# GpSimd's quarter sums in the input projection of a hybrid encoder layer, done in two runs per token block

## What is computed

```python
h = rmsnorm(x, norm1_w)
proj = h @ w_in                        # q, k, v, z, xBC, dt_f, dt_b
q = rmsnorm(q per head, q_norm_w) * 64 ** -0.5
k = rmsnorm(k per head, k_norm_w)
att = neighbourhood_attention(q, k, v, rpb)
xBC = silu(depthwise_conv(xBC, conv_w, conv_b))      # five taps
ssm = two-way chunked scan over xBC, gated by silu(z)
x = x + concatenate([att, ssm]) @ w_out
h2 = rmsnorm(x, norm2_w)
y = x + (silu(h2 @ w_gate) * (h2 @ w_up)) @ w_down
```

## Time and profile before

| | |
|---|---|
| median of 3 executions | 3426.62 us (3421.67 to 3434.69) |
| the profiled execution | 3428.72 us, of which its span is 3426.6 us |
| TensorE busy | 3205.6 us, 94% |
| VectorE, ScalarE, GpSimd busy | 2031.9 us (59%), 1390.9 us (41%), 720.0 us (21%) |
| granted TensorE clock, mean over the span | 0.972 |
| input projection | from the start to about 790 us |

### The profile page before, as it was taken

One profiled execution on the slowest core, in us unless ns is written; L12 is line 12 of the kernel. 1 busy time (PEld: TensorE's weight loads), 2 busy tenths in 40 slices (PEclk: granted clock), 3 DMA queues, 4 the chain that ended last, 5 costly groups with the idle time before them and its releaser, 6 DMA issues. The chain is left out here.

```text
span 3426.6 us, 48500 instructions
## 1 busy us (share of the span) xinstructions
PE 3205.6 (94%) x16456; PEld 2762.9 (81%) x16456; DVE 2031.9 (59%) x3070; ACT 1390.9 (41%) x2610; POOL 720.0 (21%) x683
## 2 busy tenths in 40 slices
PE   7999999996999779979979999999999998999999
PEld 6877777774777558968858999999999997887887
DVE  3446556473666578974447555755576665555655
ACT  3333434354667535542214333433343333434443
POOL 5453534412333236742220000000000000000000
PEclk9999999998999989989989999999999999999999
DMA  8686858567433032236656454745475555666776
GB/s 267 232 292 219 327 179 330 201 232 132 87 83 75 29 86 68 66 128 197 204 183 229 148 162 150 235 151 159 150 227 175 174 174 201 215 220 236 272 248 214
DMA packets 458415, 630.02 MB, mean 184 GB/s; under 512 B 133120, under 2 KB 271920, under 8 KB 453856
## 3 DMA queue, kind: packets, MB, share of 16 engines
q1 hardware_dynamic: 431808, 522.36, 48.0%
q0 software_dynamic: 23600, 100.80, 8.4%
q10 hardware_dynamic: 2880, 5.24, 0.4%
HBM read 451.25 MB, written 177.75 MB: 184 GB/s over the span
## 5 line engine op out<-in xcount | busy, mean ns | idle before, releaser
L65 PE MATMUL u_acc<-u_h_hi,u_w_hi 128*128 128x448 f32 (+1 forms) x1848 | 657.5, 356 | 23.9 <-DVE u_h_lo L2333 21.4
L66 PE MATMUL u_acc<-u_h_lo,u_w_hi 128*128 128x448 f32 (+1 forms) x1848 | 656.9, 355 | 0.0
L67 PE MATMUL u_acc<-u_h_hi,u_w_lo 128*128 128x448 f32 (+1 forms) x1848 | 656.8, 355 | 0.0
L65 PEld LDWEIGHTS u_acc<-u_h_hi,u_w_hi 128*128 128x128 f32 x1848 | 348.0, 188 | 44.3 <-issue 22.9
L67 PEld LDWEIGHTS u_acc<-u_h_hi,u_w_lo 128*128 128x128 f32 x1848 | 347.9, 188 | 18.5
L66 PEld LDWEIGHTS u_acc<-u_h_lo,u_w_hi 128*128 128x128 f32 x1848 | 348.0, 188 | 18.3
L2577 ACT CAST d_hi<-d_raw 128x896 fp32r<-128x896 f32 (+1 forms) x231 | 225.0, 983 | 279.4 <-PE d_acc L67 140.9
L460 DVE TENSOR_TENSOR i_w_lo<-i_raw,i_w_hi 128x2048 fp32r<-128x2048 f32 x60 | 158.0, 2633 | 295.7 <-ACT i_w_hi L332 295.7
L65 PE MATMUL d_acc<-d_hi 128*128 128x512 f32 x770 | 302.0, 392 | 17.2 <-DVE d_lo L2598 13.0
L2598 DVE TENSOR_TENSOR d_lo<-d_raw,d_hi 128x896 fp32r<-128x896 f32 (+1 forms) x231 | 252.0, 1132 | 111.1 <-ACT d_hi L2577 105.7
L66 PE MATMUL d_acc<-d_lo,d_hi 128*128 128x512 f32 x770 | 301.4, 391 | 0.0
(11 more groups left out here) (256 smaller groups left out, 6411.4 us busy)
## 6 DMA issues: line engine op xcount, KB each, us to landing
u_w_lo<-w_ops SPq DMA_DIRECT2D x264, 256.0 KB, 2.9
i_raw<-w_in_dram SPq DMA_DIRECT2D x60, 1024.0 KB, 6.8
u_w_raw<-w_ffn_dram SPq DMA_DIRECT2D x198, 256.0 KB, 3.1
d_raw<-wd_ops SPq DMA_DIRECT2D x132, 256.0 KB, 5.7
d_raw<-hid_ops SPq DMA_DIRECT2D x154, 192.0 KB, 6.1
d_raw<-w_down_dram SPq DMA_DIRECT2D x99, 256.0 KB, 5.7
i_ops<-w_ffn_dram POOLq DMA_DIRECT2D x44, 512.0 KB, 6.3
w_ops<-i_ops POOLq DMA_DIRECT2D x22, 1024.0 KB, 6.9
```

The costliest lines, as they stand in the source:

```text
L65: pe.matmul(out, w_hi, x_hi, start=first, stop=False, skip_group_check=resumed)
L66: pe.matmul(out, w_hi, x_lo, start=False, stop=False, skip_group_check=resumed)
L67: return pe.matmul(out, w_lo, x_hi, start=False, stop=last, skip_group_check=resumed)
```

## The change

GpSimd's pieces of a block stand in two runs. `OPS_AT` gives begin, middle and end for each block. The pieces from `begin` to `middle` stand where the seven stood; then GpSimd waits until bank 3 holds v, that is until slot 7's matmuls are done, and only then makes those from `middle` to `end`. The gains of q still follow behind all of them. The runs are 4 + 4, 4 + 3, 4 + 3, 4 + 3 and 4 + 0 pieces instead of 7, 7, 7, 7 and 5. Nothing is computed otherwise.

```diff
-    OPS = 7
+    OPS_AT = ((0, 4, 8), (8, 12, 15), (15, 19, 22), (22, 26, 29), (29, 33, 33))
...
             def token_block(tb, more, conv):
-                for n in range(OPS * tb, min(OPS * (tb + 1), 3 * FP)):
+                begin, middle, end = OPS_AT[tb]
+                for n in range(begin, end):
+                    if n == middle:
+                        pool.wait_ge(acc_ready[3], tb * USES + USE[6] + 1)
                     if n + 1 < 3 * FP:
                         load_ops(n + 1)
                     make_ops(n)
```

## The result

| | before | after |
|---|---|---|
| median | 3430.7 us (4 runs) | 3483.0 us (4 runs, 3470.3 to 3489.9) |
| ratio | | 1.0157, 95% interval 1.013 to 1.0184 |
| profiled execution, its span | 3428.7, 3426.6 us | 3487.1, 3485.0 us |
| granted TensorE clock | 0.972 | 0.965 |

A forecast was written before the change was run, and what follows sets the result against it. TensorE, busy 94% of the span, bounds the kernel. Stalls 61.5 plus restarts 8.8 minus saving 19.2 give +51.1 us on 3428.7, that is 3479.8; less 2.1 to the median, 3477.7 us, 8 times in 10 within 3453 to 3505.

The forecast's parts named there:

- The saving: Blocks 1 to 3, slot 7 to slot 10: no piece beside the taps, waits for v and clock loss gone, 19.2 us.
- The stalls: TensorE waits at slot 10 for q's first gain: 12.6 us in blocks 1 to 3, 23.7 in block 0, together 61.5.
- Landings: GpSimd waits between pieces behind the wait for stores to land: 6.5, 4.5 and, in block 0 alone, 4.0 us.
- meetings with `w_lo`: Slots 8 to 10: VectorE's `w_lo` lengthens GpSimd's sums, charged 3.0 us, one full meeting and half of another.
- The port rule: VectorE instructions with two SBUF inputs and GpSimd instructions reading SBUF exclude each other; slots 8 to 10, 5.8 us of meetings.
- my third rival: Every `w_lo` meets a sum in full, 2.8 us more in each of four blocks: 3488.9 us, chance 0.15.
- The clock: TensorE's restarts at the low clock level after the waits at slot 10: four at 2.2 us, 8.8 us.
- In block 4 the wait for v: TensorE's wait for v in block 4, 2.6 us, stays after the change.
- The first: The gains don't gate slot 10, or are in time: -19.2 us, 3407.4 us, chance 0.03.
- The second: Short stalls, +24 us, partly paid back by four later waits for `h_lo` vanishing: 3439 us, chance 0.06.
- The fourth: Landings stay as long as in the busy slots or longer, the high end: 3533 us, chance 0.06.

The follow-up runs named there:

- Run 1: The changed order, but GpSimd's multiplication of q by its gains left out and VectorE counting up `ev_ready`; 3416.0 us, ratio 0.9956 against the kernel before.
- run 4: The changed kernel with one piece behind the wait in blocks 1 to 3 and block 0 left whole; 3412.5 us, ratio 0.9952 against the kernel before.
- run 5: The changed kernel with two pieces behind the wait in blocks 1 to 3 and block 0 left whole; 3413.8 us, ratio 0.9958 against the kernel before.
- run 10: The changed kernel with four pieces put beside the taps in blocks 1 to 3 and every piece's sums left out; 3405.5 us, ratio 0.9924 against the kernel before.
- run 8: The changed kernel again, unchanged, for a second profile; 3477.7 us in 6 runs, ratio 1.0141 against the kernel before.
- run 3: The changed kernel's numbers of pieces with the new wait taken out; 3431.1 us, ratio 0.9994 against the kernel before.
- run 7: The kernel before again, unchanged, for a second profile; 3417.9 us in one execution.

## Why the prediction was right

**The saving.** It was put at 19.2 us, all of it in blocks 1 to 3. Run 1 gave -0.44%, that is -15 us, after some 5 us given back at the start of block 1; run 4 gave -0.48%, -16 us. The first matmul of the attention came at 776.0 and 774.9 us in runs 4 and 5, against 799.7 and 789.3 before. The mechanism is shown by runs 4 and 10: freeing slot 7's taps takes the wait away, and it is the sums that lengthen the taps. The size is right for the first profile and somewhat large for the kernel as such: in its second profile the waits for v in blocks 1 to 3 were 4.8 + 2.3 + 3.5 = 10.6 us instead of 12.7.

**The stalls.** Expected 12.6 us in each of blocks 1 to 3 and 23.7 in block 0, 61.5 together; measured 12.39, 12.39, 12.59 and 23.36, 60.7. That the total hits this well is partly compensation:

- Landings, charged 6.5 + 4.5 = 11.0, took 5.53 + 4.17 = 9.7 in block 1. In block 0 they took 5.39, 4.07 and 3.87 us against 6.5, 4.5 and 4.0.
- The pieces, charged 3.0 for meetings with `w_lo`, lost 3.9 us. Block 1's first piece lasted from 298.22 to 307.73, 9.5 us instead of 7.09, and the third took 8.56. Of this the meetings are 3.4 us; the other 0.5 is the issue of the first piece's store (1.04 instead of 0.58), which ran beside VectorE's scaling of the tokens (L468) and which the prediction doesn't have.
- The port rule of the Trainium skill ("SBUF — State Buffer", "Who interferes with whom") led me to 5.8 us for three full meetings. Measured were 2.0, 0 and 1.5: two of the three `w_lo` met a sum, so my third rival, built on it, did not come. The rule itself fits the runs: one sum went from 1.28 to 3.24 us, and taking the sums away freed the taps entirely.

GpSimd's last rows in block 0, whose bracketed times are the three landings, end in the four gains:

```profile
137.37 0.53 POOL L577 DMA_DIRECT2D i_ops<-w_ffn_dram  x1 [5.39 <-DMA w_ops<-i_ops]
...
148.54 0.53 POOL L577 DMA_DIRECT2D i_ops<-w_ffn_dram  x1 [4.07 <-DMA w_ops<-i_ops]
...
161.33 0.53 POOL L577 DMA_DIRECT2D i_ops<-w_ffn_dram  x1 [3.87 <-DMA w_ops<-i_ops]
...
168.33 4.97 POOL L633 TENSOR_TENSOR i_ev<-i_ev,i_q_gain 128x512 f32<-128x512 f32 x4
```

**The clock.** Four restarts were charged 2.2 us each. In block 1 the matmul that starts at 338.86 is the tenth after the one at 334.54; ten at the full clock's 0.234 us would have taken 2.3 instead of 4.3, so 2.0 us were lost. Reckoned in the same way, blocks 0, 2 and 3 lost 2.4, 1.5 and 1.9, so that the four restarts cost 7.8 us, not 8.8.

**The sum by blocks.** From the starts of the five blocks and of the attention, as the mean of two profiles each, before 149.4, 154.5, 152.5, 154.3 and 157.9 us, after 174.5, 164.0, 162.4, 163.5 and 154.2. The differences are +25.1, +9.5, +9.9, +9.2 and -3.7, together +50; the steps of the prediction give +25.9, +8.2, +7.9, +9.1 and 0, together +51. By the medians the cost was 52.4 us, and by run 8's ratio 48. In blocks 1 and 2 less was saved than I took from one profile; block 4 made up for it. In block 4 the wait for v was 2.5 and 1.5 us before, 0.6 and 0.8 after. I had said it would stay. Why it shrank is not settled: run 3, with four pieces in block 4, had 0.7, but run 1, also with four, 1.8.

**The spans.** The two first profiles differ by 58.4 us, of which only 41.7 lie in the input projection; 15 of the rest are the gate and up products (runs 7 and 8). Read without a second profile, this would have looked like an effect of the change far downstream.

**The rivals.** The first, that the gains do not gate or are in time, falls with the 60.7 us and run 1. The second, waits for `h_lo` paid back, falls with 19.5 us of them against 18.6. The fourth, long landings, falls with landings of 3.9 to 5.8 us behind the wait in all blocks.

## What to carry to other kernels

Work moved into an engine's idle time is free only if what stands behind it in that engine's queue can still be on time: count from the event that releases it to the first result behind it that someone waits for, landings included. Here 24.0 us held two pieces and not three, and the third cost its full length. Before moving all contended work, find the one place where the contention reaches the bounding engine; freeing slot 7's taps with a single moved piece gave all of the gain that any of these orders gave.

## What the runs showed of the hardware that I had not expected

- Contention goes both ways, and in these rows who is first decides who pays. In block 1 of the changed kernel the `w_lo` at 299.96 came when a piece's sums were running one behind another: it took 5.27 us instead of 2.29, and then the last sum of the same piece, from 303.15, took 3.24 instead of 1.28. The `w_lo` at 325.03 came ahead of the next piece's first sum: it took its 2.29 us, and the sum, from 325.60, took 2.84.
- Whether a short wait costs clock varies. In the second profile of the kernel before, a wait of 2.31 us was followed by matmuls at the full clock throughout, and one of 3.53 by a first one of 0.76; in its first profile, after 4.01 us the first took 0.47 too, and the slow ones (0.63) began with the fifth. After 23.36 us of waiting the matmuls were back at the full clock 5.2 us later, a loss of 2.4, and after the 3.92 us of block 2 in the first profile before they were back 6.4 us later, a loss of 2.8. So a long wait didn't cost more restart than a short one.
- The gate and up products run at one of two speeds, 1.4% apart, in different executions of the same program, at a granted clock of 1.00 in the stretches I read in both. What decides this was not tried.
